# A fused two-block transformer kernel: level 0 interleaved with a projection, the compressed and sliding branches' small products placed within a gate slab and a projection, and the mixer's output projection begun by pairs of features

## The chip, the core and the metric

The kernel runs on 1 core of a Trainium2 chip. Its metric is device time in microseconds (us). Three runs of the kernel before took 1520.92, 1521.98 and 1523.09 us: median 1521.98 us.

The core has five engines with their own instruction queues: PE (TensorE, matrix products into PSUM), DVE (VectorE), ACT (ScalarE), POOL (GpSimd) and SP (which here only issues DMAs). They meet through semaphores.

## The reference

One sequence of 256 tokens with 1024 features runs through two blocks, in fp32.

```python
# block 1
u = rms_norm(h, norm_mix_pre)
q, kc, vc, ks, vs, kw, vw, g, q_s, k_s, v_s, gate_a, gate_b = split(u @ w_in)
o_a = g0 * compressed_attention(q, gelu(blocks(kc) @ w1_k) @ w2_k, ...) \
    + g1 * selected_attention(...) + g2 * window_attention(...)   # 8 heads of 64
o_b = sliding_attention_with_sinks(q_s, k_s, v_s)                 # window 128
y = sigmoid(gate_a) * (o_a @ w_up_nsa) + sigmoid(gate_b) * (o_b @ w_up_swa)
h = h + rms_norm(y @ w_out, ...)
h = h + rms_norm(square(relu(rms_norm(h) @ w_mlp_in)) @ w_mlp_out, ...)
# block 2
xa, qkv, z, beta, a, gate_a, gate_b = split(rmsnorm(h) @ w_in_2)
y_a = pool_mixer(xa) @ w_pool_up
# gated delta rule, 8 heads of 128, chunks of 64 tokens:
lower = strict(k_beta k^T * decay);  t_inv = inverse(I + lower)
u, w = t_inv v_beta, t_inv (k_beta * exp(gc))
# ... a state carried over 4 chunks, then
y_b = (rmsnorm(o) * silu(z)) @ w_dn_up
h = h + (sigmoid(gate_a) * y_a + sigmoid(gate_b) * y_b) @ w_mix_out
h = h + peer_ffn(rmsnorm(h))     # product keys: 8 heads x 16 experts of 16384 per token
out = rmsnorm(h, final_norm)
```

With 256 tokens all four 64-token blocks are always among the selected ones, so the selected branch is plain causal attention.

## The kernel before, in words

Every queue is an order written out by hand. A weight slab is 128 x 4096 fp32 (2 MB); 53 slabs pass through a ring of three. SP loads slab n when the slab that stood in its place has been read, that is, when the PSUM bank of its last product is full (`slab_read`).

**Split weights.** From the first product to the 6 `qkv` slabs each product of block 1 and of `qkv` is done as three products of rounded parts (`three`, line 538 on): a slab is cut in two halves, ACT rounds a half (`weight_high(h)`, line 1620), POOL forms what is left (`weight_low(h)`, line 1999), and `take_half` makes PE wait for half `h` to have been formed. One half (`DVE_HALF`, of the second mixer slab) is formed by DVE (line 1270). Half 4 and half 5 belong to the slab `v_att`; `split_rows("v_att")` goes through half 4, then half 5. Other products are plain fp32 (`feature_major`, `up_proj`).

**Attention in block 1.** Six attention units run one behind another, each as `att_scores` (PE), softmax (DVE, ACT), `att_T` (transposes), `att_out`. Between them PE takes a gate or projection slab as cover. The last such slab is `gate_b1`, of two banks with two column blocks of 24 products each. Before it stand `cmp_k` and `cmp_v` (the compressed keys and values); behind it, each waiting for the step ahead of it on another engine, `att_T(5)`, `cmp_scores` (16 products with 16 moving columns), `att_out(5)`, the transposes of `o_swa`, the transposes of the compressed probabilities (`cmp_pT`), `cmp_out`, then the projection `up_swa` (8 column blocks of 4 products), the transposes of `o_nsa`, and `up_nsa`.

**Mixer in block 2.** ACT makes decay rows out of PSUM (`eR`, line 1851), DVE subtracts and clamps (lines 1366 to 1369), ACT takes two exponentials (1855, 1857), POOL multiplies three times (2030 to 2034): by the strict mask, by `beta_r2`, by the other mask. ACT's queue does this group by group for four groups, and behind them drains the two banks of `gate2_b1`, then copies `k_tok` and `v_tok`. DVE scales those (1378 to 1381) and drains the products `kk` and `kq` (1389, 1391). PE then runs the slab `z0` and behind it **level 0**: POOL masks a group into `level_L` (two buffers, line 2049), PE transposes it (829), DVE adds the identity to both (1403, 1405). Group 2 can be masked only when group 0 is drained. Levels 1 to 5 follow with POOL's next masks.

**End of the mixer.** `dn_up` ends in four banks; DVE multiplies and adds each pair of features into `mixed2_T` (1475, 1477) and signals once, behind the fourth. PE waits for that with all of `mix_out`.

**Experts.** POOL gathers 16 x 16 rows per token tile through indirect DMAs, DVE takes dot products, PE adds the rows up. This lasts from some 840 us to the end.

The kernel's code that the diff touches, with the profile's line numbers:

## Time and profile before

| | |
|---|---|
| median of 3 runs | 1521.98 us |
| the profiled execution | 1521.91 us |
| its span, first to last instruction | 1520.0 us |
| PE busy | 1339.7 us (88%) |
| DVE busy | 864.2 us (57%) |
| POOL busy | 657.7 us (43%) |
| ACT busy | 470.5 us (31%) |
| mean granted TensorE clock | 0.948 |
| DMA moved | 389.90 MB |

Times inside the execution count from the first instruction. A timeline row merges neighbours of one kind; a plain fp32 product shows as two records, so x48 is 24 products. The figure behind "idle before" is how long the engine stood still ahead of the row, and the arrow says who released it.

### The profile page before, as it was taken

What the parts mean: (1) busy time and instruction counts of PE and PEld (TensorE: products, weight loads), DVE (VectorE), ACT (ScalarE), POOL (GpSimd) and SP (SyncE); (2) the same over time, 40 slices, a digit from 0 to 9 for tenths busy, and PEclk for the clock granted to TensorE, in tenths of its full rate; (3) what the DMA queues carried; (4) which work ended last, traced back from release to release, by engine and by line L of the source; (5) the groups of instructions that cost most, each with busy time, mean ns of one, the idle gap of its engine ahead of it and who ended that gap; (6) DMA issues with size and microseconds to landing.
All of it is one profiled execution on the core that took longest, in us unless ns stands there. A gap on an engine that the chain in (4) does not pass through costs nothing.

```text
span 1520.0 us, 17428 instructions
## 1 busy us (share of the span) xinstructions
PE 1339.7 (88%) x6390; PEld 962.3 (63%) x6390; DVE 864.2 (57%) x1684; ACT 470.5 (31%) x807; POOL 657.7 (43%) x393
## 2 busy tenths in 40 slices
PE   5999998999989998899999798689778988877876
PEld 5897977998869998899685454244334443323332
DVE  2143252799335956322332876777676677676654
ACT  3564423443344523122101222222222222222211
POOL 5543227788856614221000644444344445444430
PEclk9999899999999999999999899999899999999998
DMA  7624414445443442130133899999999999999993
GB/s 266 247 96 172 155 62 160 167 167 207 181 166 112 166 169 81 56 111 1 56 111 111 360 421 422 421 421 421 422 422 421 421 422 421 421 422 420 421 421 137
DMA packets 50043, 389.90 MB, mean 257 GB/s; under 512 B 5144, under 2 KB 9384, under 8 KB 10024
## 3 DMA queue, kind: packets, MB, share of 16 engines
q0 software_dynamic: 36864, 268.45, 42.5%
q1 hardware_dynamic: 10560, 116.40, 20.3%
q10 hardware_dynamic: 2536, 3.95, 0.8%
q8 instruction: 51, 0.84, 0.2%
q14 instruction: 32, 0.26, 0.1%
HBM read 387.70 MB, written 1.07 MB: 256 GB/s over the span
## 4 chain that ended last, share of the span: by engine, by line
PE 27%; DMA 26%; DVE 5%; POOL 2%; issue 1%; ACT 1%; DVEq 0%; POOLq 0%; ACTq 0%
PE psum L488 27%; DMA work<-experts_dram,work 14%; DMA weight_ring<-experts_dram,work 10%; DVE work L1551 2%; DMA constants<-experts_dram,work 1%; POOL work L2071 1%; ACT work L1935 0%; POOL weight_ring L2071 0%; ACT work L1620 0%; DVE work L1523 0%; DVE work L1524 0%; POOL work L2049 0%; DVE work L1538 0%; DVE work L1540 0%; DVE work L1381 0%
## 5 line engine op out<-in xcount | busy, mean ns | idle before, releaser
L488 PE MATMUL psum<-work 128*128 128x128 f32 (+6 forms) x1740 | 455.4, 418 | 87.6 <-ACT work L1935 82.7
L488 PEld LDWEIGHTS psum<-work 128*128 128x128 f32 (+2 forms) x1740 | 255.8, 195 | 277.9 <-issue 160.3
L1999 POOL TENSOR_TENSOR weight_lo<-weight_ring,weight_hi 128x2048 fp32r<-128x2048 f32 x65 | 304.2, 4680 | 193.7 <-ACT weight_hi L1620 159.3
L2071 POOL DMA_INDIRECT work<-experts_dram,work x154 | 172.3, 1119 | 241.3 <-PE psum L488 203.5
L1551 DVE CUSTOM_DVE_ANT_0 work<-work 128x1024 f32<-128x1024 f32 x154 | 189.2, 1228 | 114.0 <-DMA work<-experts_dram,work 99.6
L488 PE MATMUL psum<-weight_ring,work 128*128 128x512 f32 (+1 forms) x444 | 192.2, 581 | 33.9 <-ACT work L1935 32.3
L488 PEld LDWEIGHTS psum<-weight_ring,work 128*128 128x128 f32 (+1 forms) x444 | 79.9, 184 | 137.0 <-issue 81.0
L488 PE MATMUL psum<-normed_T,weight_ring 128*128 128x256 f32 (+1 forms) x768 | 158.0, 365 | 2.0 <-ACT normed_T L1620 1.1
L488 PEld LDWEIGHTS psum<-normed_T,weight_ring 128*128 128x128 f32 x768 | 137.1, 193 | 24.8 <-issue 6.7
L1620 ACT ACTIVATE weight_hi<-weight_ring 128x2048 fp32r<-128x2048 f32 x66 | 125.7, 1912 | 82.6 <-PE psum L488 48.2
L488 PE MATMUL psum<-mlp_in_hi,weight_hi 128*128 128x256 f32 x504 | 145.5, 289 | 6.2 <-POOL weight_lo L1999 5.5
L1935 ACT ACTIVATE work<-constants,work 128x128 f32<-128x128 f32 x256 | 102.8, 401 | 153.1 <-DVE work L1565 144.6
L488 PE MATMUL psum<-mlp_in_lo,weight_hi 128*128 128x256 f32 x504 | 144.3, 286 | 0.0
L488 PE MATMUL psum<-mlp_in_hi,weight_lo 128*128 128x256 f32 x504 | 144.3, 286 | 0.0
L1551 DVE CUSTOM_DVE_ANT_0 work<-work,weight_ring 128x1024 f32<-128x1024 f32 x79 | 96.8, 1225 | 65.5 <-DMA weight_ring<-experts_dram,work 57.9
L2071 POOL DMA_INDIRECT weight_ring<-experts_dram,work x79 | 92.4, 1170 | 95.0 <-PE psum L488 85.5
L1620 ACT ACTIVATE work<-psum 128x512 f32<-128x512 f32 (+6 forms) x111 | 64.1, 577 | 180.8 <-PE psum L488 149.6
L488 PEld LDWEIGHTS psum<-mlp_in_hi,weight_hi 128*128 128x128 f32 x504 | 98.6, 196 | 8.5 <-POOL weight_lo L1999 5.9
L1926 ACT ACTIVATE work<-work,norm_stats 128x4 f32<-128x4 f32 (+1 forms) x65 | 19.3, 297 | 269.4 <-DVE work L1551 264.0
L488 PEld LDWEIGHTS psum<-mlp_in_lo,weight_hi 128*128 128x128 f32 x504 | 98.5, 195 | 0.0
L488 PEld LDWEIGHTS psum<-mlp_in_hi,weight_lo 128*128 128x128 f32 x504 | 98.5, 195 | 0.0
L488 PE MATMUL psum<-work,weight_ring 128*128 128x256 f32 x320 | 70.0, 380 | 1.1 <-ACT work L1620 1.1
(259 smaller groups left out, 1711.4 us busy)
## 6 DMA issues: line engine op xcount, KB each, us to landing
weight_ring<-weights_dram SPq DMA_DIRECT2D x52, 2048.0 KB, 7.9
work<-experts_dram,work POOLq DMA_INDIRECT x154, 21.5
weight_ring<-weights_dram SPq DMA_DIRECT2D x2, 1024.0 KB, 13.4
gain_rows<-gains_dram SPq DMA_DIRECT2D x2, 1024.0 KB, 10.1
work<-bias_rows_dram ACTq DMA_DIRECT2D x2, 1024.0 KB, 10.4
weight_ring<-experts_dram,work POOLq DMA_INDIRECT x79, 19.3
constants<-constants_dram ACTq DMA_DIRECT2D x1, 1094.0 KB, 9.6
residual<-x_dram SPq DMA_DIRECT2D x1, 1024.0 KB, 5.5
```

Of the source, the lines that this page charges most:

```text
L488: return nc.tensor.matmul(o, l, r, start=start, stop=stop)
L1551: V.tensor_tensor_reduce(out=dot_junk, in0=xn[:, t, :], in1=slots[expert_slot[m]][:, 0:D], scale=1.0, scalar=0.0, op0=ALU.mult, op1=ALU.ad ...
L1620: return A.activation(out_, in_, ACT.Copy, scale=scale)
L1926: A.activation(acts[:, par, lo:hi], dots[:, par, lo:hi], ACT.Gelu, scale=token_scale(n)).then_inc(S("gelu_ready"), 1)
L1935: A.activation(diags[:, m % DIAGS, :], C("ident"), ACT.Copy, scale=coef[:, par, i:i + 1]).then_inc(S("diag_ready"), 1)
L1999: G_.tensor_tensor(low, loaded, high.bitcast(F32), ALU.subtract).then_inc(S("weight_lo_ready"), 1)
L2071: G_.indirect_dma_start(out=slots[s], out_offset=None, in_=experts, in_offset=bass.IndirectOffsetOnAxis(ap=expert[:, n % UNIT_BUFS, i:i + ...
```

## The change

It has six parts.

1. `DVE_HALVES = (5, QKV_HALF + 1)`: half 5, the second half of `v_att`, is formed by DVE ahead of its first softmax and no longer by POOL.
2. `split_features` gets hooks between its column blocks, and `gate_b1` uses them: `cmp_k` and `cmp_v` go behind its first block, `att_T(5)` behind its second, and `att_out(5)`, `cmp_scores` and the `o_swa` transposes behind its third. DVE combines unit 5 before it reads `cmp_scores`; ACT drains `gate_b1` in two parts. `o_swa_T` lies where `q_swa` was.
3. `up_proj` gets such hooks too, and `up_swa` uses them: `cmp_pT` behind block 0, `cmp_out` behind block 2, the `o_nsa` transposes behind block 6.
4. ACT makes all four groups of `eR` before the first clamped exponential. POOL's multiplication by `beta_r2` goes; DVE's drain of `kk` takes it over, as four 128-column operations in place of one of 512.
5. The transposes of level 0 go behind the two banks of `z0`, two groups each.
6. `mixed2_ready` is signalled for each pair of features, and the first `mix_out` waits pair by pair.

```diff
-DVE_HALF = QKV_HALF + 1
+DVE_HALVES = (5, QKV_HALF + 1)
...
-    o_swa_T = view(work, 17408, 4, SEQ)
+    o_swa_T = view(work, 10240, 4, SEQ)
...
-                if h == DVE_HALF:
-                    pe.wait_ge(S("mixer_weight_lo_ready"), 1)
+                if h in DVE_HALVES:
+                    pe.wait_ge(S("vector_weight_lo_ready"), DVE_HALVES.index(h) + 1)
...
                 for i in range(2):
+                    if 2 * i in between:
+                        between[2 * i]()
                     hi, lo = take_half()
                     ps = open_bank(name, i)
                     for a in range(min(2, groups - 2 * i)):
+                        if a and 2 * i + a in between:
+                            between[2 * i + a]()
...
+            split_features("gate_b1", between={1: compressed_kv, 2: lambda: att_T(5), 3: compressed_scores})
...
-            up_proj("up_swa", o_swa_T, 4)
-            pe.wait_ge(S("o_nsa_ready"), TT)
-            transposes("o_nsa_T", o_nsa, 2)
+            up_proj("up_swa", o_swa_T, 4, {1: compressed_probs_T, 3: compressed_out, 7: o_nsa_transposes})
...
+            def first_level(i):
+
+                for G in (2 * i, 2 * i + 1):
+                    pe.wait_ge(S("level_L_ready"), G + 1)
...
+            feature_major("z0", uT, KC, between=first_level)
...
-            pe.wait_ge(S("mixed2_ready"), 1)
...
                 for k in ks:
+                    if half == t == 0 and k % 2 == 0:
+                        pe.wait_ge(S("mixed2_ready"), k // 2 + 1)
...
+            def vector_weight_low(h):
+
+                dve.wait_ge(S("weight_hi_ready"), h + 1)
+                loaded, low, high = half_views(h)
+                V.tensor_tensor(low, loaded, high.bitcast(F32), ALU.subtract).then_inc(S("vector_weight_lo_ready"), 1)
+                landed(dve, "vector_weight_lo_ready")
+
+            vector_weight_low(DVE_HALVES[0])
...
-                free(V.tensor_tensor(Dm[:, u, :], ps, Dm[:, u, :], ALU.mult), "kk", G)
+                t, h0 = G // 2, (G % 2) * 4
+                for a in range(4):
+                    last = V.scalar_tensor_tensor(out=Dm[:, 4 * G + a, :], in0=ps[:, a, :], scalar=beta_r2[:, t, h0 + a:h0 + a + 1],
+                                                  in1=Dm[:, 4 * G + a, :], op0=ALU.mult, op1=ALU.mult)
+                free(last, "kk", G)
...
                 landed(act, "decay_rows_copied")
+            for G in range(4):
                 act.wait_ge(S("clamped_ready"), G + 1)
...
-                pool.wait_ge(S("strict_done"), G + 1)
-                G_.tensor_tensor(Dm[:, u, :], Dm[:, u, :], bc(beta_r2[:, t, h0:h0 + 4], [P, 4, P], 2), ALU.mult)
...
-                    sp.wait_ge(S("mixed2_ready"), 1)
+                    sp.wait_ge(S("mixed2_ready"), 4)
```

How PE's row changes between the end of `gate_b1` and `w_out` (128x16 is `cmp_scores`, 128x64 is `att_out(5)`, the rows from constants are transposes, 128x512 is `cmp_out`, 128x256 from the weight ring `up_swa` and then `up_nsa`). Before:

```order
L612 MATMUL psum<-constants,work 128x128 x8
L488 MATMUL psum<-work 128x16 x16
L488 MATMUL psum<-work 128x64 x8
L503 MATMUL psum<-constants,work 128x128 x8
L701 MATMUL psum<-constants,work 128x128 x2
L488 MATMUL psum<-work 128x512 x2
L488 MATMUL psum<-work,weight_ring 128x256 x32
L503 MATMUL psum<-constants,work 128x128 x8
L488 MATMUL psum<-work,weight_ring 128x256 x32
```

After, around `cmp_scores` within `gate_b1` (the rows from mlp_in_hi and mlp_in_lo are products of the gate):

```order
L488 MATMUL psum<-mlp_in_hi,weight_lo 128x256
L488 MATMUL psum<-work 128x64 x8
L488 MATMUL psum<-work 128x16 x16
L503 MATMUL psum<-constants,work 128x128 x8
L488 MATMUL psum<-mlp_in_hi,weight_hi_63 128x256
L488 MATMUL psum<-mlp_in_lo,weight_hi_63 128x256
```

And after, from the last product of `gate_b1` on:

```order
L488 MATMUL psum<-mlp_in_hi,weight_lo 128x256
L488 MATMUL psum<-work,weight_ring 128x256 x4
L714 MATMUL psum<-constants,work 128x128 x2
L488 MATMUL psum<-work,weight_ring 128x256 x8
L488 MATMUL psum<-work 128x512 x2
L488 MATMUL psum<-work,weight_ring 128x256 x16
L503 MATMUL psum<-constants,work 128x128 x8
L488 MATMUL psum<-work,weight_ring 128x256 x36
```

The first four groups of before have gone up into `gate_b1`, where dense products stand on both sides of them; `cmp_pT`, `cmp_out` and the `o_nsa` transposes now stand between column blocks of `up_swa`.

PE's row around `z0` and level 0 in the difference of the two (128x256 is `z0`, the rows from constants are level 0's transposes, 128x128 from work on both sides the products before and behind):

```order
 L488 MATMUL psum<-work 128x128 x32
-L488 MATMUL psum<-normed_T,weight_ring 128x256 x32
-L829 MATMUL psum<-constants,work 128x128 x16
+L488 MATMUL psum<-normed_T,weight_ring 128x256 x16
+L851 MATMUL psum<-constants,work 128x128 x8
+L488 MATMUL psum<-normed_T,weight_ring 128x256 x16
+L851 MATMUL psum<-constants,work 128x128 x8
 L488 MATMUL psum<-work 128x128 x48
```

Half of level 0's transposes stand in the middle of `z0`.

ACT's row at the decay rows before (512 columns out of PSUM is `eR`, the two from work are the exponentials):

```order
L1851 ACTIVATE work<-psum 128x512
L1855 ACTIVATE work<-work 128x512
L1857 ACTIVATE work<-work 128x512
L1851 ACTIVATE work<-psum 128x512
L1855 ACTIVATE work<-work 128x512
L1857 ACTIVATE work<-work 128x512
```

And after:

```order
L1887 ACT_TABLE_LOAD
L1887 ACTIVATE work<-psum 128x512 x4
L1892 ACTIVATE work<-work 128x512
L1894 ACTIVATE work<-work 128x512
L1892 ACTIVATE work<-work 128x512
L1894 ACTIVATE work<-work 128x512
```

Three of the four `eR` have moved ahead of the exponentials.

## Rows read from the trace of the kernel before

**Rows 1.** The page's chain that ended last, by engine, share of the span.

```profile
PE 27%; DMA 26%; DVE 5%; POOL 2%; issue 1%; ACT 1%; DVEq 0%; POOLq 0%; ACTq 0%
```

**Rows 2.** Windows, experts: length, busy PE, PEld, DVE, ACT, POOL; PEclk, DMA, GB/s.

```profile
840.00:1480.00 640.00, 521.43 (x1286) 246.38 (x1287) 444.62 (x1135) 171.28 (x385) 293.15 (x260) 0.93 1.01 419
```

**Rows 3.** Timeline, half 5 on each engine, and DVE's own half at 445.

```profile
44.89 1.91 ACT L1620 ACTIVATE weight_hi<-weight_ring 128x2048 fp32r<-128x2048 f32 x1
...
46.95 9.19 POOL L1999 TENSOR_TENSOR weight_lo<-weight_ring,weight_hi 128x2048 fp32r<-128x2048 f32 x2 [5.47 <-ACT weight_hi L1620]
...
51.54 0.45 PE L488 MATMUL psum<-weight_hi,mlp_in_hi 128*128 128x408 f32 x1 [2.75 <-POOL weight_lo L1999]
...
445.20 2.29 DVE L1270 TENSOR_TENSOR weight_lo<-weight_ring,weight_hi 128x2048 fp32r<-128x2048 f32 x1
```

**Rows 4.** Windows at both ends of the slow stretch in `v_att`.

```profile
52.50:53.50 1.00, 1.00 (x5) 0.98 (x4) 0.00 (x0) 0.00 (x0) 1.00 (x1) 0.56 1.02 434
55.00:56.00 1.00, 1.00 (x5) 0.97 (x4) 0.00 (x0) 0.68 (x2) 1.00 (x1) 0.50 0.87 288
```

**Rows 5.** Timeline of PE, 162 to 226, and the 16-column products at 466.

```profile
162.42 3.64 PE L488 MATMUL psum<-work 64*128 64x128 f32 x32
...
167.53 0.66 PE L488 MATMUL psum<-parameters,work 128*128 128x64 f32 x4 [1.04 <-DVE work L1187]
...
182.05 6.56 PE L488 MATMUL psum<-work 64*128 64x16 f32 x48
189.52 1.94 PE L503 MATMUL psum<-constants,work 128*128 128x128 f32 x8 [0.90 <-issue]
...
192.82 3.53 PE L488 MATMUL psum<-work 128*128 128x512 f32 x4 [0.94 <-ACT work L1620]
196.19 13.98 PE L488 MATMUL psum<-work,weight_ring 128*128 128x256 f32 x64
...
212.19 14.05 PE L488 MATMUL psum<-work,weight_ring 128*128 128x256 f32 x64 [1.14 <-ACT work L1620]
...
466.28 3.41 PE L488 MATMUL psum<-parameters,normed_T 128*128 128x16 f32 x27
```

**Rows 6.** Windows, a dense gate slab and three stretches at the lower clock.

```profile
149.40:160.90 11.50, 11.50 (x97) 11.50 (x96) 0.00 (x0) 6.08 (x5) 9.69 (x3) 1.00 0.51 185
169.00:172.00 3.00, 3.00 (x16) 3.00 (x15) 1.03 (x3) 2.59 (x14) 0.00 (x0) 0.50 0.00 0
189.00:196.00 7.00, 5.54 (x14) 3.51 (x15) 2.76 (x8) 4.78 (x5) 1.15 (x1) 0.50 0.00 0
470.00:475.00 5.00, 5.00 (x24) 5.00 (x25) 4.96 (x5) 0.26 (x2) 3.31 (x1) 0.50 0.56 236
```

**Rows 7.** Timeline, from the decay rows to level 1, and a drain at 738.

```profile
590.06 1.23 ACT L1700 ACTIVATE work<-psum 128x512 f32<-128x512 f32 x2
...
590.71 1.28 PE L813 MATMUL psum<-constants,work 128*128 128x128 f32 x8 [3.30 <-ACT work L1700]
...
600.99 0.69 DVE L1389 TENSOR_TENSOR work<-psum,work 128x512 f32<-128x512 f32 x1
...
601.82 14.05 PE L488 MATMUL psum<-normed_T,weight_ring 128*128 128x256 f32 x64 [0.85 <-DVE work L1389]
...
621.18 2.70 POOL L2049 TENSOR_TENSOR work<-work,constants 128x512 f32<-128x512 f32 x2 [1.29 <-DVE work L1405]
622.76 1.65 PE L488 MATMUL psum<-work 128*128 128x128 f32 x6 [1.71 <-POOL work L2049]
...
738.01 1.12 DVE L1437 SCALAR_TENSOR_TENSOR work<-work,psum 128x128 f32<-128x128 f32 x4 [2.85 <-PE psum L488]
```

**Rows 8.** Timeline of PE, the first product of `mix_out`.

```profile
801.44 1.98 PE L488 MATMUL psum<-weight_ring,work 128*128 128x512 f32 x4 [1.58 <-DVE work L1477]
```

**Rows 9.** Windows, 24 transposes in a row.

```profile
584.00:588.00 4.00, 3.41 (x28) 3.04 (x26) 3.30 (x4) 0.59 (x2) 3.08 (x3) 1.00 0.56 156
```

**Rows 10.** Timeline of DVE beside POOL's halves of `w_out`.

```profile
195.80 4.13 DVE L1222 TENSOR_TENSOR work<-work 128x512 f32<-128x512 f32 x1
```

More of the change, by code:

```diff
@@ L505, in transposes, with feature_major @@
                             close_bank(ins, name, i)
-            def feature_major(name, moving, kcs, groups=4, after=None):
+            def feature_major(name, moving, kcs, groups=4, after=None, between=None):
                 w = take_slab().rearrange("p (k n) -> p k n", k=kcs)
@@ L682, in _ @@
-            close_bank(ins, "cmp_v")
-            split_features("gate_b1")
-            att_T(5)
-            drained(pe, "cmp_k")
-            for g in range(2):
-                ps = open_bank("cmp_scores", g)
-                for t in range(TT):
-                    for j in range(4):
-                        ins = mm(ps[:, (t * 4 + j) * 16:(t * 4 + j + 1) * 16],
-                                 q_nsa[g * HD:(g + 1) * HD, j, t * P:(t + 1) * P], cmp_k[g * HD:(g + 1) * HD, :])
-                close_bank(ins, "cmp_scores", g)
@@ L693, in _, with compressed_kv @@
-            att_out(5)
-            for name, src in (("o_swa_T", o_swa), ):
+            def compressed_kv():
+                pe.wait_ge(S("cmp_act_ready"), 1)
+                ps = open_bank("cmp_k")
+                w2k = PR("w2_k").rearrange("p (a n) -> p a n", a=2)
+                for jh in range(2):
+                    ins = mm(ps[:, 0:32], w2k[:, jh, :], cmp_act[:, 0, jh, :], jh == 0, jh == 1)
+                close_bank(ins, "cmp_k")
+                pe.wait_ge(S("cmp_rep_ready"), 1)
+                ps = open_bank("cmp_v")
+                w2v = PR("w2_v").rearrange("p (a n) -> p a n", a=2)
+                for jh in range(2):
+                    ins = mm(ps[:, 0:HD], cmp_rep[:, jh, :, :].rearrange("p h n -> p (h n)"), w2v[:, jh, :], jh == 0, jh == 1)
+                close_bank(ins, "cmp_v")
@@ new lines, in compressed_scores @@
+            def compressed_scores():
+                att_out(5)
+                drained(pe, "cmp_k")
+                for g in range(2):
+                    ps = open_bank("cmp_scores", g)
+                    for t in range(TT):
+                        for j in range(4):
+                            ins = mm(ps[:, (t * 4 + j) * 16:(t * 4 + j + 1) * 16],
+                                     q_nsa[g * HD:(g + 1) * HD, j, t * P:(t + 1) * P], cmp_k[g * HD:(g + 1) * HD, :])
+                    close_bank(ins, "cmp_scores", g)
@@ L695, in _ @@
                 for n in (2, 5):
                     drained(pe, f"att_out{n}")
-                transposes(name, src, 2)
-            pe.wait_ge(S("cmp_probs_ready"), 1)
-            ps = open_bank("cmp_pT")
-            for t in range(TT):
-                ins = nc.tensor.transpose(ps[:, t * P:(t + 1) * P], cmp_scores[:, t, :, :].rearrange("p h n -> p (h n)"), ident)
-            close_bank(ins, "cmp_pT")
-            drained(pe, "cmp_pT")
-            drained(pe, "cmp_v")
-            for t in range(TT):
-                ps = open_bank("cmp_out", t)
-                close_bank(mm(ps[:, :], cmp_pT[:, t, :], cmp_v.rearrange("p h d -> p (h d)")), "cmp_out", t)
+                transposes("o_swa_T", o_swa, 2)
@@ new lines, in _, with compressed_probs_T, compressed_out @@
+            split_features("gate_b1", between={1: compressed_kv, 2: lambda: att_T(5), 3: compressed_scores})
+            def compressed_probs_T():
+                pe.wait_ge(S("cmp_probs_ready"), 1)
+                ps = open_bank("cmp_pT")
+                for t in range(TT):
+                    ins = nc.tensor.transpose(ps[:, t * P:(t + 1) * P], cmp_scores[:, t, :, :].rearrange("p h n -> p (h n)"), ident)
+                close_bank(ins, "cmp_pT")
+            def compressed_out():
+                drained(pe, "cmp_pT")
+                drained(pe, "cmp_v")
+                for t in range(TT):
+                    ps = open_bank("cmp_out", t)
+                    close_bank(mm(ps[:, :], cmp_pT[:, t, :], cmp_v.rearrange("p h d -> p (h d)")), "cmp_out", t)
@@ L1197, in _ @@
                  "cmp_v")
+            att_factors(5)
+            att_combine(5)
             sv = cmp_scores
```

77 lines of the change are left out of this document (32 added, 45 removed).

## The prediction

> **What bounds the kernel now.** I read the page's chain that ended last first: PE has 27% of the span on it, DMA 26%, every other engine 5% or less [rows 1]. It falls in two halves. From about 840 us on the experts are gathered: over 640 us the DMA engines are busy all the time (share 1.01) at 419 GB/s [rows 2]. Those bytes are the same in both kernels, and every gather waits for a routing that follows the last product of the mixer; so this half should only slide. Before 840 us PE works nearly without a pause, and where it does not, the timeline names an engine it waits for. So the change can be priced as pauses of PE that go, plus work of PE that runs at 2.4 GHz where it ran at 1.2 GHz. Both are read from PE's timeline and from windows, whose PEclk column reads 1.00 or 0.50 for the two levels.
>
> **Part 1, half 5 to DVE.** ACT has rounded half 5 at 44.89 + 1.91 = 46.80. POOL takes 9.19 / 2 = 4.6 us for it, until 51.54, and PE stands still for 2.75 us [rows 3]. DVE has nothing to do there and needs 2.29 us for such a half (its own at 445.20) [rows 3]: 46.85 + 2.29 = 49.14, so PE resumes 2.4 us earlier, after a pause of some 0.4 us. Behind the pause of before the clock is at the lower level: 0.56 in the window from 52.5, 0.50 in the one that ends at 56 [rows 4], some 3.4 us, of which half is lost: 1.7 us. With so short a pause I take it to stay up. Sum 4.1 us. Bounds: 2.4 (the clock falls all the same) to 4.5. POOL's next half, 6, is begun when ACT has rounded it, 2.5 us earlier than before, and PE wants it 4 us earlier, at 56.5; it is ready near 53.7. The new wait stands at the head of DVE's softmax, whose scores come only at 55.
>
> A row speaks of a danger here: a 512-column DVE operation with both inputs in SBUF, 0.69 us elsewhere, takes 4.13 us beside a POOL half [rows 10, 7]. Were POOL's half 6 to start first, half 5 would come at 53.7, 2.2 us later than now. But half 6 is rounded only at 49.0, when DVE is within 0.2 us of its end.
> By the Trainium skill, SBUF — State Buffer, "Who interferes with whom", a DVE operation with two SBUF inputs and a reading GpSimd operation exclude one another, and whoever started first keeps the port to its end; the 4.13 us agree. By that rule DVE, which starts 2.2 us ahead, wins here, so the sum stays; started second it would lose the 2.2 us.
>
> **Parts 2 and 3, the end of attention.** Before, from the first small product behind `att_out(4)` at 165.9 to `up_nsa` at 212.19 are 46.3 us. What PE has to do in them, at the upper clock: `gate_b1`, 96 products as in the window of 11.5 us [rows 6], 11.5; `cmp_k` and `cmp_v` 1.0; `att_T(5)` 1.0; `cmp_scores` and `att_out(5)`, 24 products at 3.64 / 16 = 0.225 us, 5.4; the `o_swa` transposes half of 1.94, 1.0; `cmp_pT` 0.3; `cmp_out` half of 3.53, 1.8; `up_swa` 13.8; the `o_nsa` transposes 1.0 [rows 5]. Sum 36.8 us, so 9.5 us are pauses (1.04 + 0.90 + 0.94 + 1.14 = 4.0 [rows 5]) and lower clock (5.5: 0.50 at 169 to 172 and at 189 to 196 [rows 6]).
>
> Do the pauses go? I laid the new order out with these durations. Each hook's input is ready before PE comes to it: `att_T(5)` at 172.8 after exponentials that end at 171.6; `att_out(5)` at 176.7, its copies at 175.5; `cmp_pT` at 187.3, the masked probabilities at 186.3; `cmp_out` three column blocks of `up_swa` later; the `o_nsa` transposes at 199.8, DVE done at 194.5. The thinnest cover is the 1.0 us behind `cmp_probs_ready`. SP's load of the first `w_out` slab is set off by `gate_b1`'s last bank, now 4 us later on the same count, but PE wants it only after `up_nsa`. ACT's roundings of that slab stand ahead of its `o_nsa` copies and end by 198. So all 4.0 us of pauses.
>
> Does the clock stay up? Not wholly. Products with 16 moving columns keep the array little occupied: the `beta_a` group, which stands in dense work as `cmp_scores` will, runs from 466.0 to 470, and the windows behind it are at 0.50 to 475 [rows 5, 6]. `cmp_scores` is 3.3 us of such products. I charge 2.0 us (3.4 to 4 us of dense work at the lower level). Bounds: nothing lost, or twice the charge: gain 9.5 to 5.5. I take 7.5 us.
>
> **Parts 4 and 5, decay rows and level 0.** Before, ACT drains the two banks of `gate2_b1` at 590.06, behind four rounds of DVE and ACT by turns, and PE stands 3.30 us for them [rows 7]. With all `eR` first, the rounds no longer wait for each other: DVE needs at most 3.1 us a group, ACT's last exponential ends near 582, and the drains follow `gate2_b1` itself (584.8). They end at 585.5 and not 591.3, 5.8 us earlier; the `k_tok` and `v_tok` copies and DVE's scaling, in line behind them, too. The first `kk` drain begins at 595.2 and not 600.99. It now takes four operations, 1.12 us for such four at 738.01, in place of 0.69 [rows 7]: 0.4 back. PE waits for it with `z0` (0.85 before [rows 7]), so `z0` starts at 596.4 and not 601.82: 5.4 us. PE itself, done with `kq` at 595.8, is not late. The three further drains cost 0.4 each, beside `z0`.
>
> From there, before: `z0` 14.05, then 6.9 us until the first product of level 1 at 622.76, which waits for POOL [rows 7]. After: `z0` with 8 transposes (1.0) in it, then 4 transposes 0.5, DVE's 0.69, POOL's mask 1.35 (half of 2.70 [rows 7]) and hand-overs 0.2: about 2.7 us. POOL's masks of groups 2 and 3 come beside the second bank of `z0`. So 6.9 - 1.0 - 2.7 = 3.2 us. Together 8.6; a little of the lower clock stays at level 1: 8.3 us. Bounds: 6 (handovers between levels 0 and 1 stay as long as before) to 9.5. POOL's `beta_r2` step is hidden either way.
>
> A rule that speaks against these hooks is about transposes. The rows: 24 in a row, 2.8 us, from 584.6, with PEclk 1.00 [rows 9]. In the Trainium skill, TensorE: Matmul & The Clock Gate, "Part 4: PE-mode transpose", a transpose does not count as a busy PE for the clock. By the trace 8 transposes within a slab cost their 1.0 us; by the rule the slab around each would lose clock as well (rival 2).
>
> **Part 6, `mix_out`.** Its first product waits 1.58 us for DVE's last addition [rows 8]. With three pairs ready, six products (about 0.85 us each) cover it: 1.5 us. Its slabs were loaded long before. Bounds 1.0 to 1.6. SP's wait for the keys is for the fourth signal, as late as before.
>
> **Sum.** 4.1 + 7.5 + 8.3 + 1.5 = 21.4 us. The profiled execution took 1521.91 us (its span 1520.0), the median of the runs is 1521.98: 1500.5 us.
>
> **The rivals.**
> 1. DVE, not ACT, holds `z0`: its clamps run against POOL's masks, or the level 0 adds queue behind the four-part drains, and parts 4 and 5 give half. For it: DVE is the next in line on every step. Against it: none of its terms fills the 5.8 us. 1521.9 - 17.3 = 1504.6 with the other parts whole, and about 1509 if the hooks of `gate_b1` also meet a late ACT (another 4).
> 2. Transposes and small products take the clock down at each of the three new places (`o_swa` in the gate, `o_nsa` in `up_swa`, level 0 in `z0`): 1.7 us each beyond the charge, 1505.6. Against it: rows 9.
> 3. The gather does not slide: something fixed in time holds it, and only 0 to 3 us reach the end: 1520. Against it: no transfer after 840 is asked for without a product or a routing before it.
> 4. Slower: the short products in `gate_b1` and `up_swa` leave the clock at the lower level through the gate, both projections and `w_out`, some 75 us of PE work at the upper level. Each us spent at 1.2 GHz costs half a us, so from 43 us at that level on the gain is gone; through all of it (150 us) PE loses 75, and the time is about 1575. For it: `beta_a`. Against it: each low stretch in the trace ends within 10 us, most within 4.
>
> **How the numbers follow.** Forecast 0.76, rival 1 0.11, rival 2 0.06, rival 3 0.03, rival 4 0.04. The terms' lower bounds sum to 14.9 and the upper to 25.1: 1507.1 to 1496.9; a little more each way for what the clock does elsewhere, 1495.5 to 1508.5, which takes in rival 2 and the milder rival 1. Within 0.2% (3 us, what a measurement here can tell from nothing) falls rival 3; faster has 0.93, slower 0.04.
>
> **What would show it.** PE's row behind half 4 of `v_att` shows a pause under 1 us and PEclk 1.00 near 52. `up_nsa` starts 11 to 12 us earlier than 212.19. `gate_b1` has one stretch at 0.50, at or behind `cmp_scores`. `z0` starts 16 to 18 us before 601.82 and level 1 19 to 21 before 622.76. No pause ahead of `mix_out`. The first gather comes 21 us earlier and the stretch from it to the end keeps its length. A pause of 2 us or more ahead of a hook, or an end that does not follow the first gather, would make it wrong.

## The result, and the profile after

The changed kernel takes 1496.57 us, the median of 4 runs (1495.34 to 1497.60), beside 1522.00 us for the kernel before, run with it. The ratio is 0.9833, with a 95% interval of 0.9815 to 0.985. That is 25.4 us faster; 21.4 were forecast. The profiled execution took 1495.34 us (span 1493.5, mean granted clock 0.960), 26.6 us less than the profiled one of before.

**The second half slid.** The chain by engine (it could be followed further back than in [rows 1]), the experts' window moved by 24 us, and the first gather:

```profile
PE 60%; DMA 26%; DVE 6%; POOL 3%; issue 2%; ACT 1%; ACTq 0%; DVEq 0%; POOLq 0%
```

```profile
816.00:1456.00 640.00, 526.87 (x1287) 248.37 (x1288) 442.93 (x1126) 169.08 (x382) 293.51 (x259) 0.93 1.01 421
```

```profile
813.88 1.64 POOL L2105 DMA_INDIRECT work<-experts_dram,work  x1 [22.77 <-DVE work L1576]
```

DMA share 1.01 and 421 GB/s stand where [rows 2] had 1.01 and 419. The first gather came at 841.0 us and now comes 27.1 us earlier; from it to the end are 679.6 us, 679.0 before, 677.0 to 679.3 in the twelve experiments. So all that follows is about TensorE's (PE's) queue ahead of 814 us.

**Half 5.** Timeline of the changed kernel, one row from each engine, and the windows behind it (columns as in [rows 2]):

```profile
46.66 2.29 DVE L1138 TENSOR_TENSOR weight_lo<-weight_ring,weight_hi 128x2048 fp32r<-128x2048 f32 x1 [26.11 <-ACT weight_hi L1655]
...
48.92 4.59 POOL L2036 TENSOR_TENSOR weight_lo<-weight_ring,weight_hi 128x2048 fp32r<-128x2048 f32 x1 [7.71 <-ACT weight_hi L1655]
...
49.01 0.45 PE L488 MATMUL psum<-weight_hi,mlp_in_hi 128*128 128x408 f32 x1 [0.48 <-DVE weight_lo L1138]
```

```profile
52.00:56.00 4.00, 4.00 (x24) 3.52 (x23) 0.95 (x2) 2.38 (x4) 1.51 (x1) 1.00 1.07 388
```

Against [rows 3, 4]: the pause is 0.48 us instead of 2.75, and the clock stays at 2.4 GHz. POOL starts half 6 just as DVE ends half 5.

**The end of attention.** PE's timeline, 164 to 213 us:

```profile
164.73 0.53 PE L488 MATMUL psum<-work,parameters 128*128 128x32 f32 x4
...
168.49 1.04 PE L618 MATMUL psum<-constants,work 128*128 128x128 f32 x8
...
172.23 5.15 PE L488 MATMUL psum<-work 128*128 128x64 f32 x48
177.31 1.09 PE L503 MATMUL psum<-constants,work 128*128 128x128 f32 x8
...
179.27 0.41 PE L488 MATMUL psum<-mlp_in_hi,weight_hi 128*128 128x256 f32 x1
...
184.34 0.38 PE L714 MATMUL psum<-constants,work 128*128 128x128 f32 x2
...
188.01 1.88 PE L488 MATMUL psum<-work 128*128 128x512 f32 x4
...
196.64 1.04 PE L503 MATMUL psum<-constants,work 128*128 128x128 f32 x8
...
212.87 0.58 PE L488 MATMUL psum<-weight_hi,mixed_hi 128*128 128x512 f32 x1
```

No row has a bracket: all four pauses of [rows 5] are gone. `cmp_out` (188.01) takes 1.88 us where it took 3.53. One thing is left: behind the third hook a product of `gate_b1` takes 0.41 us per record instead of 0.28, and the window there reads 0.57:

```profile
178.00:182.00 4.00, 4.00 (x23) 4.00 (x22) 1.28 (x4) 2.90 (x4) 0.00 (x0) 0.57 0.00 0
```

The last column block takes 4.62 us (178.16 to 182.8), as against 3.11 for the block before it: 1.5 us lost. `w_out` begins 13.0 us earlier than the 225.9 of before.

**The mixer.** PE's timeline from the `k_tok` transposes on, then `mix_out`:

```profile
569.12 3.66 PE L835 MATMUL psum<-constants,work 128*128 128x128 f32 x32
572.61 7.31 PE L488 MATMUL psum<-work 128*128 128x128 f32 x64
580.96 7.15 PE L488 MATMUL psum<-normed_T,weight_ring 128*128 128x256 f32 x32 [1.03 <-DVE work L1422]
587.94 1.04 PE L851 MATMUL psum<-constants,work 128*128 128x128 f32 x8
588.81 7.07 PE L488 MATMUL psum<-normed_T,weight_ring 128*128 128x256 f32 x32
595.72 1.04 PE L851 MATMUL psum<-constants,work 128*128 128x128 f32 x8
598.78 11.26 PE L488 MATMUL psum<-work 128*128 128x128 f32 x96 [2.02 <-POOL work L2083]
...
774.44 4.03 PE L488 MATMUL psum<-weight_ring,work 128*128 128x512 f32 x9
```

The pause of 3.30 us in [rows 7] is gone, `z0` comes 20.9 us earlier than there (17.2 us behind the first `k_tok` transpose before, 11.8 now), level 1 another 3.1. The 1.58 us ahead of `mix_out` [rows 8] are gone too. Eight transposes within a slab take 1.04 us.

**The ledger**, from starts of the same work on PE in the two profiles: up to `q_swa` (half 5) 4.1 us; the end of attention 8.9; `w_out` and the norm behind it 0.5 given back; from the `beta_a` group to the `xa` slab 3.0 (no stretch at 1.2 GHz there, 469 to 476 us before); from `k_tok` to `z0` 5.4; level 0 3.1; level 1 1.2 (no stretch at 1.2 GHz, 619 to 626 before); `mix_out` 1.8; 0.5 given back until the end. Sum 26.5, as the spans.

### The profile page after: what moved, and what is told of

It is laid out like the page before. It is cut to its first block, busy times and chain, and to the rows that moved or that the text cites. A ratio compares the mean times of both kernels' runs of the same rounds, so it can differ in the third digit from the quotient of the medians.

```text
span 1493.5 us, 17435 instructions
## 1 busy us (share of the span) xinstructions
PE 1329.4 (89%) x6390; PEld 954.2 (64%) x6390; DVE 859.4 (58%) x1697; ACT 470.4 (31%) x807; POOL 651.2 (44%) x388
## 4 chain that ended last, share of the span: by engine, by line
PE 60%; DMA 26%; DVE 6%; POOL 3%; issue 2%; ACT 1%; ACTq 0%; DVEq 0%; POOLq 0%
PE psum L488 59%; DMA work<-experts_dram,work 14%; DMA weight_ring<-experts_dram,work 10%; DVE work L1586 2%; DMA constants<-experts_dram,work 1%; POOL weight_lo L2036 1%; POOL work L2105 1%; PE psum L618 1%; ACT work L1972 0%; POOL norm_stats L2026 0%; DMA bias_rows_dram<-work 0%; ACT work L1655 0%; DVE residual L1097 0%; POOL weight_ring L2105 0%; ACT work L1800 0%
## 5 line engine op out<-in xcount | busy, mean ns | idle before, releaser
L488 PE MATMUL psum<-work 128*128 128x128 f32 (+6 forms) x1740 | 449.8, 413 | 87.1 <-ACT work L1972 81.3
L488 PEld LDWEIGHTS psum<-work 128*128 128x128 f32 (+2 forms) x1740 | 250.5, 191 | 275.3 <-issue 160.8
L2036 POOL TENSOR_TENSOR weight_lo<-weight_ring,weight_hi 128x2048 fp32r<-128x2048 f32 x64 | 299.7, 4683 | 182.5 <-ACT weight_hi L1655 159.4
L2105 POOL DMA_INDIRECT work<-experts_dram,work x154 | 175.6, 1140 | 238.3 <-PE psum L488 202.5
L2105 POOL DMA_INDIRECT weight_ring<-experts_dram,work x79 | 88.8, 1124 | 95.4 <-PE psum L488 84.4
```

The lines of the kernel that those rows point to most:

```text
L488: return nc.tensor.matmul(o, l, r, start=start, stop=stop)
L2036: G_.tensor_tensor(low, loaded, high.bitcast(F32), ALU.subtract).then_inc(S("weight_lo_ready"), 1)
L2105: G_.indirect_dma_start(out=slots[s], out_offset=None, in_=experts, in_offset=bass.IndirectOffsetOnAxis(ap=expert[:, n % UNIT_BUFS, i:i + ...
```

## The experiments

The first four each undo one part, or two parts that belong together, and keep the rest. The experiments ran in three sets, each beside the kernel before, which took 1521.78, 1522.31 and 1521.03 us in them; ratios are to it. "Above the changed kernel" means above the 1496.57 us of its first median. A median is good to some 1 to 2 us, so terms of 1 or 2 us rest on the pauses in the traces.

### Half 5 back to POOL

```diff
-DVE_HALVES = (5, QKV_HALF + 1)
+DVE_HALVES = (QKV_HALF + 1, )
...
-            vector_weight_low(DVE_HALVES[0])
```

> The changed kernel with part 1 undone (POOL forms half 5 again). Theory: the gain is the sum of pauses and lower-clock stretches that each part takes away where it stands; part 1 is worth 4.1 us (in the changed kernel v_att's second half began 2.5 us earlier and ran its 24 products in 4.7 us and not 6.3). So the time is 1496.6 + 4.1 = 1500.7 us, PEclk near 52 us is 0.5 to 0.6 again, and the beta_a products behind the first mixer slab keep PEclk 1.00 as in the changed kernel. Rival: whether a group of short products takes the clock down depends on when in time it falls, so that undoing 4.1 us ahead of it brings back the lower clock behind beta_a (6.8 us at 0.50 before, none after, worth 2.9 us): 1503.6 us, and low windows behind beta_a.

Measured: 1501.63 us, ratio 0.9873 (0.9853 to 0.9893), 5.1 above the changed kernel. PE's row at half 5:

```profile
51.07 0.71 PE L488 MATMUL psum<-weight_hi,mlp_in_hi 128*128 128x408 f32 x1 [2.98 <-POOL weight_lo L2035]
```

The pause is back, and 3.4 us at the lower clock behind it (51 to 55). `cmp_v` comes at 168.7 instead of 165.1: 3.6 us. The term of 4.1 lies between the 3.6 of the traces and the 5.1 of the medians.

### No hooks in gate_b1 and up_swa

```diff
-            split_features("gate_b1", between={1: compressed_kv, 2: lambda: att_T(5), 3: compressed_scores})
+            compressed_kv()
+            split_features("gate_b1")
+            att_T(5)
...
-            up_proj("up_swa", o_swa_T, 4, {1: compressed_probs_T, 3: compressed_out, 7: o_nsa_transposes})
+            up_proj("up_swa", o_swa_T, 4)
```

> The changed kernel with parts 2 and 3 undone (compressed branch and transposes behind gate_b1 and up_swa as before). Theory of the sum: up_nsa starts 8.9 us later relative to att_out(4), the time is 1505.5 us, with pauses of 0.9 to 1.1 us ahead of the o_swa transposes, cmp_out and up_nsa, and 10 us at PEclk 0.50 around 182 to 192. Rival (clock by position in time): the same, but beta_a gets low windows too: 1508.4 us; or the 0.50 stretch around cmp_scores is 3.4 us longer or shorter than the 10.2 us of before.

Measured: 1506.61 us, ratio 0.9909 (0.9887 to 0.9931), 10.0 above the changed kernel; `w_out` at 221.6 instead of 212.9. The waits of PE are those of [rows 5] again:

```profile
184.35 1.94 PE L503 MATMUL psum<-constants,work 128*128 128x128 f32 x8 [0.90 <-issue]
...
187.65 3.78 PE L488 MATMUL psum<-work 128*128 128x512 f32 x4 [0.94 <-ACT work L1657]
...
207.90 4.34 PE L488 MATMUL psum<-work,weight_ring 128*128 128x256 f32 x19 [1.15 <-ACT work L1657]
```

So the hooks give 8.7 us here, 8.9 in the first pair of profiles.

### Parts 4 and 5 undone

```diff
-            feature_major("z0", uT, KC, between=first_level)
+            feature_major("z0", uT, KC)
+            first_level(0)
+            first_level(1)
...
+                G_.tensor_tensor(Dm[:, u, :], Dm[:, u, :], bc(beta_r2[:, t, h0:h0 + 4], [P, 4, P], 2), ALU.mult)
```

(the exponentials by turns and the single drain of `kk` are back too)

> The changed kernel with parts 4 and 5 undone (decay rows by turns, beta_r2 on POOL, level 0 behind z0). Theory: z0 starts 5.4 us later and level 1 another 3.1 us, and 1.3 us of lower clock come back behind the pauses: 1496.6 + 9.8 = 1506.4 us; beta_a, which stands ahead of all of it, keeps PEclk 1.00. Rival (the mixer parts are worth only what the pauses are, 8.5 us, and the clock's 1.3 us is luck): 1505.1 us.

Measured: 1506.02 us, ratio 0.9904 (0.9883 to 0.9926), 9.5 above. From the first `k_tok` transpose to `z0` 17.2 us, from there to level 1 20.9, as before.

### mix_out waits for all pairs

```diff
+            pe.wait_ge(S("mixed2_ready"), 4)
...
-                    if half == t == 0 and k % 2 == 0:
-                        pe.wait_ge(S("mixed2_ready"), k // 2 + 1)
```

> The changed kernel with part 6 undone (mix_out waits for all four pairs). Theory: one pause of 1.6 us ahead of mix_out, 1498.2 us. Rival: the pause is covered by something else once the rest has moved (the slab of mix_out or the query slab then lands last), and the time stays 1496.6 us.

Measured: 1498.94 us, ratio 0.9855 (0.9827 to 0.9882), 2.4 above. Its runs, 1495.48 to 1501.44, overlap those of the changed kernel, so it is the pause that shows the part at work:

```profile
779.48 5.85 PE L488 MATMUL psum<-weight_ring,work 128*128 128x512 f32 x13 [1.65 <-DVE work L1511]
```

The four losses add up to 27.0 us, beside 25.4 for the whole. As far as four medians of this noise can tell, the parts do not lean on each other.

This kernel has a second use. Up to the mixer's end it is the changed kernel, and its milestones up to 453.7 us are the same within 0.1 us. Yet two windows of the changed kernel and then of this one read:

```profile
456.00:464.00 8.00, 8.00 (x69) 8.00 (x69) 7.93 (x10) 1.33 (x5) 4.58 (x1) 1.00 0.55 229
601.00:607.00 6.00, 6.00 (x56) 6.00 (x56) 2.77 (x4) 1.62 (x3) 2.75 (x4) 1.00 0.24 102
```

```profile
456.00:464.00 8.00, 8.00 (x57) 8.00 (x57) 7.93 (x10) 0.64 (x3) 4.56 (x1) 0.79 0.55 231
601.00:607.00 6.00, 5.99 (x39) 5.80 (x39) 1.38 (x2) 1.19 (x2) 2.69 (x3) 0.72 0.50 212
```

The same products in the same order ran at 1.00 in one execution and partly at 0.50 in the other. The other three kernels, too, show 3.4 us at the lower clock behind `beta_a` (from 460.6, 465.7 and 456.6 us on). The theories for half 5 and for parts 4 and 5 had ruled that out, and the rivals for half 5 and for the hooks had it. But their reason, that the stretch goes by the group's place in time, does not hold: here the group stands where it does in the changed kernel, within 0.1 us.

### The changed kernel again

> The changed kernel once more, unaltered. Theory (the clock's low stretches fall by chance on or off the short-product groups): PE's row and its pauses are the same to 0.2 us up to cmp_scores, but the list of low-clock stretches before 850 us differs from the 34 us of the first profile (one or two more or fewer of 3.4 us, behind beta_a or at level 1), and the profiled span lies between 1493 and 1497 us. Rival (the stretches are fixed by where a group stands in time in this kernel): the same stretches at 178, 240, 431 and 441 us and none at beta_a and level 1, span 1493.5 us again.

Measured: 1497.66 us (1495.87 to 1500.42), ratio 0.9838 (0.9825 to 0.9852), beside 1522.31 for before: a gain of 24.7. Its profiled execution (1500.42 us) ran at 1.2 GHz longer than the first one, behind the third hook, and behind `beta_a`, where the first did not at all:

```profile
176.00:184.00 8.00, 8.00 (x47) 7.96 (x47) 1.43 (x4) 2.50 (x4) 0.00 (x0) 0.57 0.01 2
459.00:467.00 8.00, 8.00 (x44) 8.00 (x44) 7.93 (x10) 0.26 (x2) 4.54 (x1) 0.57 0.50 213
```

Summed over windows of 1 us up to 850, the lower clock held PE for 34.1 us in the first profile and 51.2 us in this one, of one and the same kernel; `mix_out` begins at 774.4 in one and 780.0 in the other. So what a single pair of profiles says of the clock is uncertain by some us, and the profiled execution of the changed kernel (the fastest of four) was a lucky one. The stretches of the rival, the same as in the first profile, did not come. The theory had other stretches right, but its span of 1493 to 1497 us was exceeded (1497.9), and PE comes to `cmp_k` 0.8 us later, not within 0.2.

### Scores of 64 columns

The key block is repeated four times, so each of the 16 `cmp_scores` products moves 64 columns instead of 16; DVE reads the first 16.

```diff
-                             q_nsa[g * HD:(g + 1) * HD, j, t * P:(t + 1) * P], cmp_k[g * HD:(g + 1) * HD, :])
+                             q_nsa[g * HD:(g + 1) * HD, j, t * P:(t + 1) * P],
+                             cmp_k[g * HD:(g + 1) * HD, :].unsqueeze(1).to_broadcast([HD, 4, 16]))
...
```

> The changed kernel with cmp_scores at 64 moving columns and not 16: each product's moving operand, the compressed keys, is repeated four times over, and the drain reads the first 16 columns of each. Same count of products. Theory (16-column products take the clock down, since the array sees few columns): the group takes as long as before (3.3 us, the weight loads set it) and the 3.4 us at PEclk 0.50 in gate_b1's last block, at 178 to 182 us, are gone: that block takes 3.1 us and not 4.6, and the time is 1.5 us less, 1495.1 us. Rival (the transposes of att_T(5) and o_swa, or the 64-column att_out, take it down): the low stretch stays and the time is 1496.6 us.

Measured: 1497.46 us, ratio 0.9843 (0.9827 to 0.9859), beside 1497.66 for the changed kernel in the same set: no gain, and the stretch stayed:

```profile
176.00:180.00 4.00, 4.00 (x26) 3.93 (x26) 1.21 (x4) 1.59 (x3) 0.00 (x0) 0.66 0.02 4
```

That the 16 columns alone take the clock down here, the reason that the prediction gave for its charge, has fallen.

### DVE's order turned round, level 0 within the banks

DVE drains `kk` and `kq` before it scales `k_tok` and `v_tok`, and does level 0's additions between them; the transposes come in the middle of each `z0` bank, not behind it.

```diff
                         f = (2 * i + a) * P
+                        if between and a:
+                            between(i)
...
```

> The changed kernel with level 0's transposes behind z0's column blocks 0 and 2 (and not behind its two banks), and with DVE draining kk and kq ahead of the scaling of k and v, the level 0 additions of groups 0 and 1 between the scalings, and the q multiplication last. Theory: z0 no longer waits for a kk drain (1.03 us in the changed kernel) and level 1 no longer waits for POOL's mask behind the last drain (2.02 us), since one column block of z0 (3.5 us) covers it: 3.0 us less, 1493.6 us. Rival (DVE is full here: 16 us of work between kk and level 1): the additions come late, PE waits within z0 before block 3, and the time stays within 0.5 us of 1496.6.

Measured: 1493.29 us, ratio 0.981 (0.9795 to 0.9825), 3.3 below the changed kernel's first median and 4.4 below the one of the same set. PE's rows at `z0` and level 1:

```profile
583.25 3.62 PE L488 MATMUL psum<-normed_T,weight_ring 128*128 128x256 f32 x16
...
599.75 1.16 PE L488 MATMUL psum<-work 128*128 128x128 f32 x8 [0.77 <-POOL work L2096]
601.25 0.94 PE L488 MATMUL psum<-work 128*128 128x128 f32 x6 [0.34 <-POOL work L2096]
```

The wait ahead of `z0` (1.03) is gone, those at level 1 fell from 2.02 to 1.11: `z0` stands 10.6 us behind the first `k_tok` transpose and level 1 16.5 behind `z0` (11.8 and 17.8 in the changed kernel). So what PE still waited for in the changed kernel came mostly from the order of DVE's and PE's queues and not from DVE's load. Which of the two orders gave how much was not taken apart.

### The reordering and the wide scores together, with beta_a at 64 columns too

```diff
-                            ins = mm(ps[:, t * 16:(t + 1) * 16], uT[:, k, t * P:(t + 1) * P], w[:, k, :], k == 0, k == KC - 1)
+                            ins = mm(ps[:, t * 64:(t + 1) * 64], uT[:, k, t * P:(t + 1) * P],
+                                     w[:, k, :].unsqueeze(1).to_broadcast([P, 4, 16]), k == 0, k == KC - 1)
...
```

> The reordered kernel together with 64 moving columns in cmp_scores and in the beta_a group. Theory: the gains add up, 3.0 + 1.5 us and on average some 1.7 us behind beta_a, which no longer ever has a low stretch: 1490.5 us, and PEclk 1.00 behind both groups. Rival: only the reordering counts, 1493.6 us.

Measured: 1492.41 us, ratio 0.981 (0.9796 to 0.9823). That is between the theory's 1490.5 and the rival's 1493.6, and 0.9 below the reordering alone, less than a median can tell. No lower clock behind `beta_a`; the stretch behind `cmp_scores` stayed, as in the row below. And the same kernel once more:

> The kernel of e8 unchanged, beside e9 on the same chip. Theory: its time is within 0.1% of 1492.4 (1490.9 to 1493.9); its milestones on TensorE up to cmp_scores are those of e8 within 0.8 us; the low-clock stretches differ by one or two of 3.4 us each, as between the two profiles of the changed kernel (34.1 and 51.2 us in all before 850 us), so that mlp_in and mix_out begin up to 4 us from e8's 247.2 and 772.0. Rival (the stretches are fixed by the program's instructions): all stretches before 850 us again sum to 34.1 us, and mix_out begins at 772.0 within 0.5.

Measured: 1490.65 us (1490.05 to 1491.46), ratio 0.9801 (0.9787 to 0.9814): the lowest median of this study, 0.2 us below the range that was expected. Its interval lies below those of the changed kernel, 0.9815 to 0.985 and 0.9825 to 0.9852, though that of the same kernel's first runs touches the former. The window behind the third hook, in the first profile of this kernel and in the second:

```profile
176.00:180.00 4.00, 4.00 (x24) 3.93 (x24) 1.14 (x3) 1.56 (x3) 0.00 (x0) 0.63 0.02 4
```

```profile
176.00:180.00 4.00, 4.00 (x36) 3.93 (x36) 1.43 (x4) 1.71 (x3) 0.00 (x0) 1.00 0.01 4
```

One execution has the stretch, the other not, and `w_out` begins 1.2 us earlier without it. The stretches before 850 us sum to 30.7 us and not to 34.1: they are not fixed by the instructions, and the rival falls.

Over all profiles of kernels with the hooks: behind 16-column scores the stretch is there in 8 of 8, behind 64-column scores in 2 of 3 (a fourth has the scores split up, next). Behind a `beta_a` of 16 columns it is there in 10 of 11 profiles, counting the kernel before and the one without hooks, and behind one of 64 in 0 of 3. So the wide `beta_a` went with the upper clock in three profiles of three; for `cmp_scores` it stays open whether the width does anything.

### The small group cut up

```diff
-            split_features("gate_b1", between={1: compressed_kv, 2: lambda: att_T(5), 3: compressed_scores})
+            split_features("gate_b1", between={1: compressed_kv, 2: unit_5_T, 3: unit_5_out})
+            compressed_scores(1)
...
-            up_proj("up_swa", o_swa_T, 4, {1: compressed_probs_T, 3: compressed_out, 7: o_nsa_transposes})
+            up_proj("up_swa", o_swa_T, 4, {2: compressed_probs_T, 4: compressed_out, 7: o_nsa_transposes})
```

> Against e8: the small group of gate_b1 (25 products of 64 or fewer columns and 8 transposes back to back) is cut up: the compressed scores of the first group of heads go to the second hook, beside the transposes of half 5; the attention output and the o_swa transposes stay at the third; the scores of the second group come behind gate_b1's last slab; the compressed probabilities and outputs follow one column block later in up_swa; ACT drains gate_b1's second bank ahead of the compressed exponentials. Theory (it is the length of the group that takes TensorE's clock down, since wider scores did not change it): no stretch of about 3.4 us at 0.50 between 172 and 186 us, w_out's first product 1.5 us earlier than e8's 212.5, time 1490.9 against e8's 1492.4. Rival (any short product among the dense ones does it): the stretch stays or moves by some us, w_out at 212.5 or later, time 1492.4 or above. Second rival: the second scores come too late for the exponentials and up_swa's hook waits for the probabilities by 1 us or more, 1493.5.

Measured: 1498.42 us, ratio 0.9854 (0.9839 to 0.9869), 7.8 above the uncut kernel on the same chip. No theory saw that. The clock did stay at 1.00 from 160 to 201 us, but so it did in the uncut kernel's second profile, so this tells nothing. The loss is in the rows of POOL, DVE and PE:

```profile
190.96 9.45 POOL L2059 TENSOR_TENSOR weight_lo<-weight_ring,weight_hi 128x2048 fp32r<-128x2048 f32 x2 [33.12 <-ACT weight_hi L1678]
```

```profile
192.24 3.80 DVE L1267 TENSOR_TENSOR work<-work 128x512 f32<-128x512 f32 x1
...
196.93 4.03 DVE L1267 TENSOR_TENSOR work<-work 128x512 f32<-128x512 f32 x1
```

```profile
201.88 1.94 PE L503 MATMUL psum<-constants,work 128*128 128x128 f32 x8 [4.50 <-DVE work L1275]
```

Two DVE operations of 0.69 us fell beside POOL's halves of `w_out` and took 3.80 and 4.03, 6.5 us more; the `o_nsa` transposes waited 4.50 for them, and 0.90 at the `o_swa` transposes and the lower clock from 201.8 to 205.2 came on top. In the changed kernel the same pair stands here:

```profile
191.52 0.69 DVE L1257 TENSOR_TENSOR work<-work 128x512 f32<-128x512 f32 x1
```

```profile
192.80 9.14 POOL L2036 TENSOR_TENSOR weight_lo<-weight_ring,weight_hi 128x2048 fp32r<-128x2048 f32 x2 [34.84 <-ACT weight_hi L1655]
```

DVE ended 0.6 us before POOL began; over all eleven profiles with the hooks and the group left whole, this margin is 0.4 to 1.4 us, and both additions take 0.69 or 0.70. In the kernel before, both operations had been caught (4.13 us [rows 10], and 4.03 for its twin), behind a whole `up_swa` that hid all but the last 1.1 us. By the Trainium skill, SBUF — State Buffer, "Who interferes with whom", whoever issues first keeps the shared pair for the whole instruction; the 3.80 and 4.03 us agree.

### Parts 4 and 5 taken apart

```diff
-            feature_major("z0", uT, KC, between=first_level)
+            feature_major("z0", uT, KC)
+            first_level(0)
+            first_level(1)
```

> The changed kernel with level 0 of the tree taken out of z0's slabs: both groups of pairs come behind z0, as before; the decay rows, the four-part drains and mix_out's pairs stay. Theory (parts 4 and 5 are two gains): z0 begins when the changed kernel's does, 11.9 us behind the first k_tok transpose (569.1 to 581.0), and level 1 begins 3.1 us later behind z0, 20.9 us instead of 17.8; the time is 3 us above the changed kernel's, 1499.6. Rival (level 0 within z0 only moves a wait that DVE and POOL set): level 1 begins 17.8 to 18.8 us behind z0, and the time is within 1 us of 1496.6.

Measured: 1499.28 us, one run. The changed kernel itself took 1495.34 to 1500.42, so this time alone decides nothing; the rows do. `z0` stands 11.8 us behind the first `k_tok` transpose and level 1 20.9 behind `z0`, as the theory said. Level 0 within `z0` is worth 3.1 us.

```diff
-            for G in range(4):
                 act.wait_ge(S("clamped_ready"), G + 1)
```

> The changed kernel with the decay rows by turns again (each group's eR right before its masks, as before); level 0 within z0, the four-part drains and mix_out's pairs stay. Theory: TensorE waits some 3.3 us for the drains of gate2_b1 again, as before at 590.71, and z0 begins 17.2 us behind the first k_tok transpose as before (584.6 to 601.8) instead of 11.9, level 1 stays 17.8 us behind z0; the time is 5.4 us above the changed kernel's, 1502.0. Rival (the gain of z0 comes from the drains and copies in another order and not from the rows): z0 at 11.9 to 13 us, time within 1.5 us of 1496.6.

Measured: 1502.42 us, one run. The time is the one the theory gave, but not for its reason: of the 7.1 us over the first profiled execution of the changed kernel (1495.34), 3.9 were lost ahead of `k_tok`, where this execution had more of the lower clock (6.8 us behind the third hook, 3.4 behind `beta_a`; 3.4 and none in the changed kernel's first profile). `z0` stands 14.5 us behind the first `k_tok` transpose, neither 17.2 nor 11.9 to 13, level 1 17.8 behind `z0`, and the pause for the drains of `gate2_b1` is 0.16 us, not 3.3. What is in between shows in ACT's and DVE's rows of one round, first with all of parts 4 and 5 undone:

```profile
557.00 0.63 ACT L1890 ACTIVATE work<-work 128x512 f32<-128x512 f32 x1 [1.75 <-DVE work L1403]
...
562.20 0.63 ACT L1890 ACTIVATE work<-work 128x512 f32<-128x512 f32 x1 [3.42 <-DVE work L1403]
```

```profile
559.66 1.21 DVE L1402 TENSOR_SCALAR work<-work 128x512 f32<-128x512 f32 x1
560.79 1.31 DVE L1403 TENSOR_SCALAR work<-work 128x512 f32<-128x512 f32 x1
```

and then here, where only the exponentials are by turns:

```profile
560.44 0.63 ACT L1891 ACTIVATE work<-work 128x512 f32<-128x512 f32 x1 [1.74 <-DVE work L1400]
...
564.58 0.63 ACT L1891 ACTIVATE work<-work 128x512 f32<-128x512 f32 x1 [2.36 <-DVE work L1400]
```

```profile
563.10 1.05 DVE L1399 TENSOR_SCALAR work<-work 128x512 f32<-128x512 f32 x1
564.07 0.41 DVE L1400 TENSOR_SCALAR work<-work 128x512 f32<-128x512 f32 x1
```

A round takes 5.2 us with POOL's three multiplications and 4.1 with two; the two clamp operations together take 2.52 and 1.46, which is the difference. One takes 0.41 us with POOL idle and 1.0 to 1.3 beside it. Three rounds follow the first: about 3.1 us on ACT's path, of which the four-part drain takes 0.4 back, and 17.2 becomes 14.5. Putting `eR` in front on top of that turns 14.5 into 11.8.

These two shares hold for this order of steps only. In the changed kernel ACT has its last exponential behind it at 564.3 us and then stands still until PE has filled the second bank of `gate2_b1`:

```profile
563.72 0.61 ACT L1894 ACTIVATE work<-work 128x512 f32<-128x512 f32 x1
...
569.38 0.60 ACT L1735 ACTIVATE work<-psum 128x512 f32<-128x512 f32 x1 [3.13 <-PE psum L488]
```

Only the last two of the four pairs of clamps run beside POOL there, in 1.82 and 1.75 us. With a third multiplication on POOL they would take 2.52, together 1.5 us more. This is an estimate from the rows above, and less than the 3.13 us that ACT has to spare; POOL's masks, too, end 12 us before DVE drains the first `kk`. So with `eR` in front, the multiplication by `beta_r2` could probably have stayed on POOL at no cost, and DVE would have kept its single drain, which is 0.4 us shorter. No run tests this.

## Why the prediction was right, step by step

- **The frame** held: gather, clock and bytes of the second half unchanged, every microsecond won ahead of it kept.
- **Part 1**, 4.1 us: 4.1 in the first pair of profiles, 3.6 in the trace and 5.1 by the medians when it is undone. Pause 0.48 against "some 0.4", clock up.
- **Parts 2 and 3**, 7.5 us: 8.9, and 8.7 by undoing them. All four pauses went, as laid out. The charge for the clock was 2.0 and came to 1.5; the rest is the step "9.5 us are pauses and lower clock", low by about 1 us. The reason for the charge (16 columns) is not borne out; the stretch is there in most executions, its cause is open, and that the charge fitted is luck. The thinnest cover was not where the prediction saw it (behind `cmp_probs_ready`) but between DVE's two additions into `o_nsa` and POOL's `w_out` halves, 0.6 us; it held.
- **Parts 4 and 5**, 8.6 us less 0.3: 5.4 and 3.1 measured, 8.5. The steps held too. The drain of `gate2_b1` now waits for PE and no longer for the rounds; the first `kk` drain begins 10.6 us and `z0` 11.8 us behind the first `k_tok` transpose, as laid out (595.2 and 596.4 less 584.6). One sentence is half wrong: "POOL's `beta_r2` step is hidden either way". In the new order it probably would be, by the 3.13 us above. In the old order it was not: POOL's multiplications hold up DVE's clamps, on which ACT's rounds wait, and taking one away alone won 2.7 us net. The Trainium skill has it in SBUF — State Buffer, "Who interferes with whom": `tensor_scalar` can enter a two-port mode that excludes GpSimd; 0.41 against 1.0 to 1.3 us agrees. The clamps beside POOL in the trace of before, 1.2 and 1.3 us long, would have shown it. The sum didn't need this sentence, since the end of `gate2_b1` on PE bounds the new order.
- **Part 6**, 1.5 us: the pause of 1.58 went; undoing it brought 1.65 back and 2.4 by the medians.
- **Transposes** (rival 2): 8 within a slab cost 1.04 us, and behind those of `att_T(5)` and `o_nsa` the clock stayed at 1.00 in all eleven profiles with the hooks and the group left whole. `o_swa`'s stand ahead of the slow stretch at the third hook, with 24 small products. Behind those of `z0` the first profile shows 1.00, but in 4 of the 7 profiles of kernels with level 0 between `z0`'s banks 3.4 us at the lower clock begin within level 1 (601.8 to 605.2 with `mix_out` waiting for all pairs), behind eight transposes and a pause of 2.0 us. With the transposes in the middle of the banks and pauses of 1.1 us it is 0 of 4. Whether pause or transposes matter was not tested, so the rule found no support at two places and is open at the third.
- **Rival 1** came in part (PE waits 1.03 us for DVE's drain, 0.85 before) and cost nothing against the forecast. Rivals 3 and 4 didn't come: the lower clock held for 34 to 51 us in all, beside 61.4 before.
- **Short by 4.0 us.** The gain of the two profiles exceeds the forecast by 5.1: parts 2 and 3 by 1.4, parts 4 and 5 by 0.2, part 6 by 0.3, lower clock that this execution didn't have between `beta_a` and level 1 by 4.2, less the 1.0 given back. The medians keep 4.0 of it (3.3 in the second set of runs). The 4.2 no part of the change explains: executions of the same code had those stretches and hadn't. How much of the medians' surplus is of this kind isn't settled. The gain of 25.4 lies beyond the 25.1 to which the upper bounds of the terms add up; the range held it only by its margin for the clock elsewhere. The signs that carry a number missed on the same side: `up_nsa` starts 13 us earlier (11 to 12 were named), `z0` 20.9 (16 to 18), level 1 24.0 (19 to 21), the first gather 27.1 (21).

## What to carry to other kernels

Price a change as pauses that go, each from its own row, and keep the clock as a separate term with a range: two profiles of one kernel differed by 17 us at the lower clock. Before calling an operation on POOL hidden, look at what DVE does beside it: an operation that nobody waits for can still double or triple the DVE operation that somebody does wait for. Then look whether that somebody has time to spare: undoing two steps one by one gives each a share, but either alone might have given nearly all. When small work moves into cover, check the new neighbours of DVE's two-input operations, not only whether each input is ready; 0.6 us decided between nothing and 4.5 us here.

## What the runs showed of the hardware

- Lower clock comes and goes between executions of the same order of work: at 176 to 180 us 0.63 and 1.00, at 456 to 464 us 1.00 and 0.79. Behind `beta_a` with 16 columns it was there in 10 of 11 profiles, with 64 in none of 3.
- DVE's clamp (one SBUF input, 128 x 512) takes 0.41 to 0.43 us alone and 1.0 to 1.3 beside POOL's multiplications; a two-input addition 0.69 alone and 3.8 to 4.1 beside a POOL half of 4.6 us.
